# When GpSimd asks for expert rows, and behind which tile it makes low parts, in a PEER expert layer

## The reference, cut to what matters

```python
def peer_ffn(h, w_q, keys, u_tab, v_tab):            # h: 512 x 1024
    q = (h @ w_q).reshape(B, S, PEER_HEADS, 2, PEER_DK_HALF)      # 8 heads, 2 halves of 128
    s = jnp.einsum('bshpd,hpkd->bshpk', q, keys)                  # 128 keys a half
    s_top, i_top = lax.top_k(s, K)                                # K = 16
    ...                                                           # 16 best of the 256 sums: idx, gate = softmax
    u_sel = jnp.take(u_tab, ix, axis=0)                           # 16384 experts, rows of 1024
    act = gelu(jnp.einsum('thkd,td->thk', u_sel, hx))
    v_sel = jnp.take(v_tab, ix, axis=0)
    return jnp.einsum('thk,thkd->td', gx * act, v_sel)
```

## Time and profile before

| | |
|---|---|
| Profiled execution | 3269.77 us; its span from first to last instruction is 3268.0 us |
| Median of three runs | 3264.67 us |
| PE busy | 3100.4 us, 95% of the span |
| DVE, POOL, ACT busy | 2621.6, 2104.2, 1329.9 us |
| Mean granted TensorE clock | 0.982 of 2.4 GHz |
| DMA | 883 MB, mean 270 GB/s |
| U tiles of layer 1 | 2009.9 to 2720.6 us; V tiles to 3254.5 us |

### The profile page before, as it was taken

One profiled execution on the slowest core, in us unless ns is written; L12 is line 12 of the kernel. 1 busy time (PEld: TensorE's weight loads), 2 busy tenths in 40 slices (PEclk: granted clock), 3 DMA queues, 4 the chain that ended last, 5 costly groups with the idle time before them and its releaser, 6 DMA issues. The chain is left out here.

```text
span 3268.0 us, 57829 instructions
## 1 busy us (share of the span) xinstructions
PE 3100.4 (95%) x21401; PEld 2657.5 (81%) x21401; DVE 2621.6 (80%) x4442; ACT 1329.9 (41%) x2376; POOL 2104.2 (64%) x1368
## 2 busy tenths in 40 slices
PE   8998998899999999899999898999999998999998
PEld 3336887789989999788888677899999997888886
DVE  8765664679988885899899666799888857999997
ACT  0124453333336775333333423333367753333333
POOL 1213443467777666888888504677776668888884
PEclk9999998999999999999999999999999999999999
DMA  9950002478778999999999514787799999999995
GB/s 344 327 175 21 4 16 85 162 259 274 259 237 311 351 374 364 363 351 349 364 352 350 208 46 159 247 272 260 234 312 350 380 361 349 351 350 362 353 352 173
DMA packets 379234, 883.09 MB, mean 270 GB/s; under 512 B 39497, under 2 KB 208001, under 8 KB 370690
## 3 DMA queue, kind: packets, MB, share of 16 engines
q1 hardware_dynamic: 284546, 536.14, 46.9%
q0 software_dynamic: 94464, 343.97, 29.4%
HBM read 780.21 MB, written 98.62 MB: 269 GB/s over the span
## 5 line engine op out<-in xcount | busy, mean ns | idle before, releaser
L1910 PE MATMUL peer_acc<-peer_hhi,peer_uhi 128*128 128x352 f32 x2048 | 678.4, 331 | 34.8 <-POOL peer1same_ulo L2141 17.7
L1910 PE MATMUL peer_acc<-peer_hlo,peer_uhi 128*128 128x352 f32 x2048 | 666.5, 325 | 0.0
L1910 PEld LDWEIGHTS peer_acc<-peer_hhi,peer_uhi 128*128 128x128 f32 x2048 | 391.2, 191 | 38.1 <-POOL peer1same_ulo L2141 18.7
L2203 DVE SCALAR_TENSOR_TENSOR peer_row<-peer_row,peer_acc 128x1024 f32<-128x1024 f32 x320 | 386.0, 1210 | 40.8 <-DMA peer_row<-in_pe_u,peer_idx 40.6
L2141 POOL TENSOR_TENSOR peer0same_ulo<-peer_u,peer_uhi 128x1024 fp32r<-128x1024 f32 x128 | 309.0, 2415 | 166.4 <-ACT peer_uhi L1995 165.7
L2141 POOL TENSOR_TENSOR peer1same_ulo<-peer_u,peer_uhi 128x1024 fp32r<-128x1024 f32 x128 | 309.3, 2418 | 164.9 <-ACT peer_uhi L1995 164.2
L1910 PEld LDWEIGHTS peer_acc<-peer_hlo,peer_uhi 128*128 128x128 f32 x2048 | 390.4, 191 | 1.0 <-issue 0.5
L2172 POOL TENSOR_TENSOR peer1lsame_vlo<-peer1l_v,peer1l_vhi 128x1024 fp32r<-128x1024 f32 x128 | 310.0, 2422 | 73.1 <-ACT peer1l_vhi L2040 72.7
L2172 POOL TENSOR_TENSOR peer0lsame_vlo<-peer0l_v,peer0l_vhi 128x1024 fp32r<-128x1024 f32 x128 | 309.3, 2417 | 71.1 <-ACT peer0l_vhi L2040 70.5
L1910 PE MATMUL peer_acc<-peer_hhi,peer1same_ulo 128*128 128x352 f32 x1024 | 333.3, 325 | 0.0
L1910 PE MATMUL peer_acc<-peer_hhi,peer0same_ulo 128*128 128x352 f32 x1024 | 333.2, 325 | 0.0
(11 more groups left out here) (488 smaller groups left out, 7067.0 us busy)
## 6 DMA issues: line engine op xcount, KB each, us to landing
peer_u<-in_pe_uT SPq DMA_DIRECT2D x256, 512.0 KB, 7.2
peer0l_v<-in_pe_v SPq DMA_DIRECT2D x128, 512.0 KB, 6.2
peer1l_v<-in_pe_v SPq DMA_DIRECT2D x128, 512.0 KB, 5.9
activations<-peer_gel SPq DMA_DIRECT2D x256, 176.0 KB, 7.4
rw_g<-in_ada POOLq DMA_DIRECT2D x60, 512.0 KB, 5.5
routing<-peer0m_wb SPq DMA_DIRECT2D x24, 1024.0 KB, 11.8
peer0l_wt<-routing SPq DMA_DIRECT2D x64, 384.0 KB, 7.6
routing<-peer1m_wb SPq DMA_DIRECT2D x24, 1024.0 KB, 11.9
```

Source lines behind the costliest of these rows:

```text
L1910: mm = pe.matmul(ub[e % 2][:, 0:UD], a, h[:, k, 0:UD], start=(n == 0), stop=(n == 3 * KT - 1))
L2203: v.scalar_tensor_tensor(out=row[:, m % NG], in0=row[:, m % NG], scalar=1.0, in1=h_own if mine else h_g, op0=ALU.mult, op1=ALU.mult, accum ...
```

## The change

It changes the order in which POOL issues, a few places on SP, ACT and PE, and no arithmetic.

1. POOL sends at most two U rows behind each low part (`AT_ONCE`), instead of as many as the bounds let through. The first rows may go from tile 10 (before: 11), those of the last head from tile 64 (before: 63). Nine rows behind tile 11 become two behind each of tiles 10 to 17; six behind tile 63 become two behind each of 64 to 69. All other tiles send what they sent.
2. V's first ten rows go one behind each of tiles 118 to 127. In the V tiles two go behind V tiles 0 and 1, and one behind each after, one row less far ahead than before.
3. `low_query` stands behind `low_u` of tiles 7n+4 and 7n+6 instead of 7n+5 and 7n+7.
4. The last head's `move_idx` on SP is behind tile 60 instead of 58.
5. PE transposes the first two groups ahead of tile 65 and the third behind it; ACT takes the third behind tile 65's gelu.

```diff
+MOVE_LAST, ROWS_AT, ROW_LEAD, AT_ONCE = 4, 4, 4, 2
 def ready_by(e):
             if heads < 2:
-                return TOPK * heads
+                return TOPK if e >= HEAD_TILES + NH else 0
             if heads < HEADS - 1:
                 return FIRST_DOTS + HEAD_DOTS * min(heads, HEADS - 2)
-            return MIXED - HEAD_OWN if e < AT_BETWEEN + 2 * IDX_LAG - 1 else DOTS
-        def rows_by(e):
-            return min(max(0, 2 * (e - AT_LAST - DOTS_END - 1)), EARLY_ROWS)
+            return MIXED - HEAD_OWN if e < AT_BETWEEN + MOVE_LAST + 1 + NH else DOTS
...
-                    if r == 2 and 1 <= n <= HEADS:
+                    if r == (2 if n < HEADS else MOVE_LAST) and 1 <= n <= HEADS:
                         move_idx(n - 1)
...
+                def turn_slots(q):
+                    for t in range(DT):
+                        mm = pe.transpose(four[q % 2][:, t * P:(t + 1) * P], slots[:, q, t], const["ident"][:])
+                    mm.then_inc(slots_turned, 1)
                     if e == AT_BLOCKS - TURN_AT + 1:
                         pe.wait_ge(slots_made, 1)
-                        for q in range(3):
-                            if q == 2:
-                                pe.wait_ge(slotT_made, 1)
-                            for t in range(DT):
-                                mm = pe.transpose(four[q % 2][:, t * P:(t + 1) * P], slots[:, q, t], const["ident"][:])
-                            mm.then_inc(slots_turned, 1)
+                        turn_slots(0)
+                        turn_slots(1)
                     u_product(e)
+                    if e == AT_BLOCKS - TURN_AT + 1:
+                        pe.wait_ge(slotT_made, 1)
+                        turn_slots(2)
...
+                def take_slots(q):
+                    act.wait_ge(slots_turned, q + 1)
+                    a.activation(slotT[:, q], four[q % 2][:, 0:SD], ACT.Copy).then_inc(slotT_made, 1)
                     if e == AT_BLOCKS - TURN_AT + 1:
-                        for q in range(3):
-                            act.wait_ge(slots_turned, q + 1)
-                            a.activation(slotT[:, q], four[q % 2][:, 0:SD], ACT.Copy).then_inc(slotT_made, 1)
+                        take_slots(0)
+                        take_slots(1)
                     tile_step(e)
                     if e == AT_BLOCKS - TURN_AT + 1:
+                        take_slots(2)
                         act.wait_ge(slotT_made, 3)
...
                 for e in range(ET):
                     low_u(e)
-                    n, r = divmod(e - 1 - NH, HEAD_TILES)
+                    n, r = divmod(e - NH, HEAD_TILES)
                     if 0 <= n < HEADS - 1 and r in (1, 3):
                         low_query(n + 1, r // 2)
-                    if e >= HEAD_TILES + 2:
-                        ready = ready_by(e)
-                        while n_u < min(NG + dots_by(e - FETCH_LAG), ready):
+                    for _ in range(AT_ONCE):
+                        if e >= FETCH_LAG and n_u < min(NG + dots_by(e - FETCH_LAG), ready_by(e)):
                             fetch_u(n_u)
                             n_u += 1
-                    if e >= AT_LAST + DOTS_END + FETCH_LAG:
-                        while n_v < NG + rows_by(e - FETCH_LAG):
-                            fetch_v(n_v)
-                            n_v += 1
+                    if e >= AT_LAST + ROWS_AT:
+                        fetch_v(n_v)
+                        n_v += 1
...
                     g.tensor_tensor(vlo[:, q], vr[:, q], vhi[:, e % NH].bitcast(F32), ALU.subtract).then_inc(vlo_made, 1)
-                    while n_v < min(NG + (rows_after(e - FETCH_LAG) if e >= FETCH_LAG else EARLY_ROWS), SLOTS):
-                        fetch_v(n_v)
-                        n_v += 1
+                    for _ in range(AT_ONCE):
+                        if n_v < min(rows_after(e) + ROW_LEAD, SLOTS):
+                            fetch_v(n_v)
+                            n_v += 1
```

## The result

The changed kernel takes 3216.74 us, the median of four runs (3213.32 to 3220.54), against 3266.68 us for the kernel before (four runs, 3264.59 to 3273.3). The ratio is 0.9844, with a 95% interval of 0.9832 to 0.9855. The profiled executions are 3269.77 and 3220.54 us, spans 3268.0 and 3218.8. So it is faster by 50 us, as forecast in sign. The forecast was 73 us, and 3216.7 lies outside its range of 3178 to 3212.

A forecast was written before the change was run, and what follows sets the result against it. PE was taken as the bound, with holes where POOL's low parts come late and slow clock behind them. Terms of -38.0 us (layer 1) and -35.1 (layer 0), together -73.1, took 3264.7 to 3191.6 us; range 3178 to 3212.

The forecast's parts named there:

- Nine rows: U tiles 10 to 17: sending the rows two by two removes PE's wait at tile 12, -7.8 us a layer.
- the queries' low parts: Heads 2 to 7: low halves made one tile sooner remove 1.9 us lost at each query, -11.4 us a layer.
- The last head: U tiles 63 to 68: tile 64's low part comes first and PE's 6.3 us wait goes, -7.3 us a layer.
- The mask wait: Tile 66: PE gets to the masks before they are made, 2.8 us of wait a layer, bounds 0 and 5.
- Two signs of being wrong: Wrong if a wait over 4 us is left in U tiles; no expert-layer window was to have granted clock 0.50.
- V's rows in the U tiles: Tiles 118 to 127: wait at tile 126 removed, 5 us of new waits; -3.5 us in layer 1, -2.0 in layer 0.
- rival A: Rows are free for the U loads: no new waits at tiles 121 to 124, 10 us more won, 3182; chance 0.13.
- The first V tiles: V tiles 0 and 1: six rows no longer delay tile 1's low part; -8.0 us in layer 1, -6.6 in layer 0.
- rival B: DMA takes the tail's gain: U loads slip 10 us, V's loads come behind, clock falls; +14.6, 3206; chance 0.15.
- C: The queries' wait only moves to tile 7n+5 or 7n+6, or DVE's lag stays: 22.8 us not won, 3214; chance 0.07.
- D: Slower: V's loop turns to DVE's or the rows' pace; 3288 at 0.4 us a tile; chance 0.03.
- E: The change doesn't do what it says, POOL still late at the same four places: about 3262; chance 0.02.

The follow-up runs named there:

- short_dots: The changed kernel with 12 of a layer's dots, two in each of heads 2 to 7, over 128 of 1024 columns: 3207.51 us.
- four_dots: The changed kernel with four dots instead of eight in head 1, the other four done in tiles 66 to 113: 3206.6 us.
- rows_first: The changed kernel with POOL's row requests ahead of `low_query` in a tile instead of behind it: 3209.81 us.
- lowq_back: The changed kernel with the queries' low parts put back behind tiles 7n+5 and 7n+7: 3233.45 us.
- tail_back: rows_first with the last head's section as before the change (parts 4 and 5, and six rows behind tile 63): 3219.89 us.
- runs 1, 3, 4, 5 and 6: Run 1: the kernel before with only part 3 of the change, 3250.58 us. Runs 3 to 6: four_dots, rows_first, short_dots, capped_only.
- short_rows: rows_first with V's first 16 row requests of a layer fetching 512 bytes a partition instead of 4096: 3197.06 us.
- lead_2: rows_first with V's rows asked two tiles ahead of the add instead of four, one request behind each V tile: 3202.91 us.
- capped_only: The kernel before with at most two U rows behind a tile up to tile 55, beginning at tile 10: 3257.97 us.

## Why the prediction was right, and where it was wrong

*Nine rows, and the queries' low parts: right.* The 19.2 us a layer came out within 0.4, and each query is 1.96 us shorter, forecast 1.9. Only together do they come to this. Alone they give 6.2 and 9.0 us by tile 49, 15 in sum: the low half of head 2 either stands ahead of the nine rows (8.2 us of wait at tile 12) or its second half behind eight of the rows (3.0 us at the query). A sum of parts priced from one trace held here because each was priced with the other done.

*The last head: the failed step.* It is the sentence that DVE "starts head 2 about 4.7 us late" and that "the lag shrinks by about a microsecond a head and is gone at head 7". I had 39.7 us of PE's head and about 38 of DVE's work, and took the rest as slack that repays a delay. The lag is 8.8 us and constant. Two things were wrong in it. First its size: PE's head 1 is 9.5 us shorter, as I had it (9.6), but head 1's numbers come 1.0 us later than before and not 2 sooner. Less the pause of 2.9 us that DVE had at head 2, that is 7.6 us at the start of head 2 (forecast 4.7), and head 2 itself takes DVE 1.2 us longer than before. Then its decay: from there on DVE takes 39.6 us a head, all that PE gives it, with 39.2 of them busy. Head 7's numbers come 5.6 and 6.9 us later than before, counted in the head. That makes the section that waits for them win 0.4 and lose 2.3 us. *short_dots* shows that a change of DVE's work alone brings head 7's numbers in time and gives the section back, and *four_dots*, *rows_first* and *lowq_back* show that without the lag the section wins 5.3 to 7.0 us. The forecast's 7.3 was itself some 1.6 too large (*tail_back*: 5.6 and 5.7), about 3 of the 16.6 us. The mask wait, which I took at 2.8 us a layer, grew by 5.6 over both layers (2.0 to 7.6), as forecast; what I had not priced is the transposes' wait of 8.6, and the slow clock behind the pauses, at most 8.5 us over both layers. Two signs of being wrong thus came true: this wait is over 4 us in layer 1 (4.9), and a window of 5 us has a granted clock of 0.55.

What holds the lag constant is shown as far as this: the freed time comes back in small operations that end with a subtraction of POOL or just behind it, and in heads 2 to 6 of the twelve kernels and the changed one the numbers come after 43.1 to 44.4, 47.8 or 53.2 us, and after nothing between. The add of line 2254 (2256 in *short_dots*) meets a subtraction in many heads, and wherever it does, in the traces of both kernels and of runs 1, 3, 4, 5 and 6, it ends 0.28 or 0.29 us behind the end of one, whenever it began. No run moved POOL's subtractions alone, so that they hold the lag is read from the rows and not tried. Why head 1 leads into the late phase is only argued: there DVE waited for rows (4.13, 2.06 and 1.31 us in layer 1) while PE was 9 us sooner. It fits that in *four_dots* and *rows_first* head 1's numbers come after 42.0 to 43.9 and 46.8 to 49.6 us, and in the changed kernel after 54.0.

*V's rows in the U tiles: right.* 2.8 and 4.0 us for the forecast 2.0 and 3.5. The new waits at tiles 121 to 124 are 3.9 and 4.2 us in the changed kernel, forecast 5 (its sums have 4.7 and 5.2), ACT's waits for U tiles near them grew from 5.4 to 14 us (forecast 10 or more), and *short_rows* shows that they are the rows' bytes: rival A, free rows, is out. Free rows would have been worth 10.5 us in the two layers' traces, forecast 10; but 3.2 of these come from U tile 127 on, where the forecast had none. The rule that I drew from the Trainium skill, DMA: Bandwidth & Descriptors, Queues, rings and completion order, gave the same side as the measurement: the requests weren't kept behind the U loads.

*The first V tiles: a term mis-sized.* Forecast 8.0 and 6.6, measured 3.6 and 3.1. The forecast left 1.6 us of waits a layer from U tile 127 on; 6.0 are there in layer 1. V tiles 0 and 1 keep 2.2 (5.48 and 4.86 us against 4.08), most of it since two requests and a low part are a period of 4.92; the forecast had 0.2 to 0.3 and 0.6 for it. U tile 127 keeps 1.9 (5.80), a wait for DVE's first weights, and tiles 2 to 7 lose 1.9 in pieces of 0.1 to 0.4, as the loads of V's weights and gelus land late behind DMA engines that are busy 1.03 of the time from 2640 to 2676 us (0.92 from 2687 to 2705). I had priced the bytes for the U loads and not for those behind them. That is rival B's mechanism, V's loads behind the rows; *short_rows* prices it at 3.2 us over both layers, where B had 14.6 in all.

*Rivals.* C came nearest in time (3214), and one half of its sentence, "DVE's lag stays", is what happened; but it stopped the last head, not the queries, none of which waits. D and E are out: *lead_2* asks even two tiles ahead without a loss in the loop.

## What to carry to other kernels

An engine that is late needn't repay its delay out of the slack that it has when it is on time; look whether its small operations meet another engine's long ones, since then the freed time can vanish in them and the lag stays until the pattern changes. Price a gain at the place where the late engine's result is next needed by the bound one, not only where the wait was removed. And where DMA is full, price the bytes of a moved transfer against every load behind it, not only the first.

## What the runs showed of the hardware that I had not expected

- DVE's write of 128 x 32 numbers is 0.18 us alone and 2.37 beside a subtraction of POOL that began 0.07 us before it; both end together. In heads 2 to 6 of both layers of the changed kernel it takes 2.35 to 2.37. The Trainium skill, SBUF — State Buffer, SBUF: two separate sides, has a rule for the single case: the two engines share a pair of ports, and of a GpSimd operation and a VectorE operation that needs the pair (one in a 2-port mode, or one with two inputs in SBUF), whichever starts first holds it for its whole length and the other blocks. The rows agree with it as far as they go: the write begins behind the subtraction and ends with it, the two other stretched operations have two inputs in SBUF, and the dots, with one input in PSUM, stay at 1.2 us beside a subtraction. In which mode the write runs no row shows. One row doesn't fit the rule as it stands: in *short_dots* the add of line 2256, 0.42 us alone, began 0.42 us before the subtraction, while POOL was in a row request, and still ended 0.29 us behind the subtraction. What these runs add is that in a periodic order the freed time can vanish in such operations, and the late engine keeps its phase.
- A pause of PE of 3.0 us, the same in two kernels, left the granted clock at 1.00 in one and brought 0.53 in the other, at a price of 2.8 us. *capped_only* ranged over 11 us between runs; whether that pause is the cause wasn't tried.
- The kernel before takes 3279.0 us (median of nine runs) on one chip and 3265 to 3269 on three others, at a mean clock of 0.980 against 0.981 to 0.985. Medians and ratios of kernels on different chips differ by several us.
